# A second buffer for gathered rows in a decode step, and another order of the gathers

## The chip, the cores and the metric

The kernel runs on one core of a Trainium2 chip, as one launch. The metric is its time on the device in microseconds (us), the median of several runs. Engines are named as the profile does: PE (TensorE), DVE (VectorE), ACT (ScalarE), POOL (GpSimd) and SP (SyncE, which here only issues DMAs).

## The reference

One step of a one-layer hybrid decoder: one prompt of 512 tokens and 8 samples of one token each with 4096 past positions. Everything is float32.

```python
h = einsum('btd,de->bte', x, w_in)            # split: HGRN2 part, NSA part, gates
o_hg, S = hgrn2_mix(...)                      # gated linear recurrence, 8 heads of 128
# NSA, per sample: rows = cache_kv[page_table] (past 4096) + the new row
kc = compress(rows[:, :, 0], cmp_w1[0], ...)  # windows of 32 rows, step 16, two-layer net
vc = compress(rows[:, :, 1], cmp_w1[1], ...)
o_cmp, p = cmp_attention(q, kc, vc, qpos)
sel = select_blocks(p, qpos, n_blocks)        # top 16 blocks of 64 rows, per kv head
o_slc = selected_attention(q, blocks(rows[:, :, 2]), blocks(rows[:, :, 3]), sel, qpos)
o_win = window_attention(q, last 512 rows of cache_win and the new one)
o_nsa = (g0 * o_cmp + g1 * o_slc + g2 * o_win) * silu(ngate)
y = LayerNorm(ALPHA * x + concat(o_hg, o_nsa) @ w_out)
```

There are 4 kv heads of 64 with 4 queries each, a model width of 2048, and pages of 128 rows.

## The kernel before, in words

The first stages (prompt, projections) leave `oT`, the transposed outputs of both head groups, [128, 16, 520]. Its first eight columns of 520 are the HGRN2 heads; they are final before the last stage and are next read by its output matmuls. The change lies wholly in that last stage, `decode_output_phase`. It has two parts.

**Decode part.** For each sample `b` of 8 (`NB`) the past rows of the first two kinds go through the compression net. POOL gathers them by indirect DMA (`rows(b, q, par)`, L1485: four gathers of 128 x 2 KB; parity `par` 0 or 1 goes to `X[0]`, in the profile Xr, or `X[1]`, in the profile xT; `q` counts four quarters). PE transposes them in units of four (`turn(Q, u)`, L1534) into one of two PSUM banks `dtb`. ACT empties a bank into `big` (L1799), DVE makes differences (L1900, L1903). Then `product(s, n)` (L1557) runs three matmuls of 512 columns a step `s`, 16 steps a sample. I count in matmuls of `product`: **step t** of a sample's piece, 48 to a sample.

Everything else is a piece with a place in a hand-written list: `AT` gives the step, counted from the start of sample `b`'s 48, at which each engine takes the piece up in its own program order, and `LAST` that of the last sample, whose later pieces lie among the output matmuls (past step 384, each further step is two output matmuls). The pieces of one sample reach over three periods: compression's second layer ("second"), scores, weights, top 16 ("sums" to "bases"), "rows" (DVE writes the list `gi` of chosen rows, L2030), then four "fetch" and "keys" pieces, SCORES, VALUES, the window ("NEWEST", WSCORES, WVALUES) and DONE.

**Chosen rows.** `chosen(b, q)` on POOL issues eight gathers (L1501) of a quarter's rows into `KV`, of which there is one. "fetch q": when the gathers have landed, ACT copies keys to `Kc` (L1856, counts `k_c`) and DVE copies values to `Vg` (L2039 or L2041, counts `v_r`). "keys q": PE transposes `Kc` (L1662), DVE copies the result to `KgT` (L1771). `chosen(b, q)` waits for the copies of the quarter before. `Kc` also serves ACT's `bend` (L1814). POOL's order is: all row gathers of the next sample (`q` 0 to 3, each when PE has turned the old ones), then the four quarters of chosen rows.

**SP's queue** loads each sample's window when the one before is done (`window(b)`, about 1 MB in, 1 MB out), then `w_out` in four pieces of 1 MB (`weights(i)`, L1437) as `X[1]` and `X[0]` come free, then `x` and the norm's weights `gb`, which lies on `w1`'s room.

**Output part.** 16 tiles of 16 matmul pairs (`output(i, k)`, L1575) of `oT` with `w_out`, two PSUM buffers, DVE adds `x` and normalizes. `output_rows` (L1589) does the 8 samples' rows.

Of the kernel before, what the change touches and what calls it, by code (L numbers as in the profile page):

```python
# [18 lines left out]
F32 = mybir.dt.float32  # L19
# [6 lines left out]
P = 128  # L26
# [1204 lines left out]
def decode_output_phase(nc, io, keep):  # L1231
# [16 lines left out]
    NC, NQ4, TILES = D // 512, 4, 9  # L1248
    ident = const[:, C_ID:C_ID + P]
    cache = io["cache"]  # L1250
    with ExitStack() as ctx:
# [14 lines left out]
        KV, Vg = sb("KV", [P, 2, KVH, RUN]), sb("Vg", [P, NT, KVH, DH])  # L1266
        Kc = sb("Kc", [P, 2, KVH, DH])
# [46 lines left out]
        g_in, v_r, k_c, kn_r = sem("g_in"), sem("v_r"), sem("k_c"), sem("kn_r")  # L1314
# [19 lines left out]
            ("second", 2): 51, ("second", 3): 53, "fetch0": 54, "keys0": 55, "mix": 56, "acc": 57,  # L1334
            "fetch1": 63, "keys1": 64, "fetch2": 70, "keys2": 71, "fetch3": 80, "keys3": 81,
# [4 lines left out]
        LAST = {  # L1340
            "SCORES": 83, "SCALE": 85, "TURNED": 87, "VALUES": 89, "NEWEST0": 90, "NEWEST1": 91,
# [14 lines left out]
        def put(key, bank):  # L1356
            place[key], emptied[key] = (bank, had[bank]), (counts[bank], counts[bank] + 1)
            had[bank] += 1
            counts[bank] += 1

# [50 lines left out]
        def _(sp):  # L1411
# [26 lines left out]

            for b in range(NB - 1):
                window(b)  # L1440
            weights(0)
            weights(1)
# [4 lines left out]
            sp.dma_start(gb, io["ln"].unsqueeze(0).to_broadcast([P, 2, D])).then_inc(gb_in, 16)  # L1447
# [4 lines left out]
            sp.wait_ge(v_r, 4 * NB)  # L1452
            sp.dma_start(z[NQT][0:NB], io["x"][SEQ:T]).then_inc(z_in, 16)
# [17 lines left out]
        @block.gpsimd  # L1471
        def _(pool):
            pairs = cache.rearrange("g r (s d) -> (g r s) d", d=2 * KVH * DH)
            heads = cache.rearrange("g r (s d) -> (g r s) d", d=DH)
            for n in range(2):
                nc.gpsimd.memset(qbd[n][:], 0.0).then_inc(init, 1)
            nc.gpsimd.memset(pn[:], 0.0).then_inc(init, 1)
            nc.gpsimd.memset(sc[:], FORCED).then_inc(init, 1)

            def rows(b, q, par):  # L1480
                if b:
                    bank, k = place[NJ * b - 4 + q, 3 - 2 * par]
                    pool.wait_ge(tr[bank], k + 1)
                for r in range(4 * q, 4 * q + 4):
                    pool.indirect_dma_start(  # L1485
                        out=X[par][:, r, :], out_offset=None, in_=pairs,
                        in_offset=bass.IndirectOffsetOnAxis(ap=row[:, 2 * b + par, r:r + 1], axis=0),
                    ).then_inc(x_in[par][q], 16)

            def chosen(b, q):  # L1490

                if q == 0:
                    pool.wait_ge(gi_r, b + 1)
                if 4 * b + q:
                    pool.wait_ge(v_r, 4 * b + q)
                    pool.wait_ge(k_c, 4 * b + q)
                for t in (2 * q, 2 * q + 1):
                    n = P if t < NT - 1 else SL
                    for h in range(KVH):
                        a = h * NT + t  # L1500
                        pool.indirect_dma_start(  # L1501
                            out=KV[0:n, t - 2 * q, h, :], out_offset=None, in_=heads,
                            in_offset=bass.IndirectOffsetOnAxis(ap=gi[b % 2][0:n, a:a + 1], axis=0),
                        ).then_inc(g_in, 16)

            for q in range(4):
                rows(0, q, 0)
            for p in range(NB):
                if p + 1 < NB:
                    for q in range(4):  # L1510
                        rows(p + 1, q, 1)
                        rows(p + 1, q, 0)
                for q in range(4):
                    chosen(p, q)

        @block.tensor
        def _(pe):
# [45 lines left out]
            def output(i, k):  # L1563
# [4 lines left out]
                if k == 0:  # L1568
                    if i == 0:
                        pe.wait_ge(kept, 2 * NB)  # L1570
                    elif i == 1:
                        pe.wait_ge(added, 4 * NB - 1)
                    else:
                        pe.wait_ge(add_r, i - 1)
# [211 lines left out]
        def _(act):  # L1786
# [59 lines left out]
            def fetch(q):  # L1846


                def do(b):
                    act.wait_ge(g_in, 512 * b + 128 * (q + 1))  # L1850
# [5 lines left out]
                    A(Kc[:], KV[:, :, :, 0:DH], ACT.Copy).then_inc(k_c, 1)  # L1856
# [34 lines left out]
        def _(v):  # L1891
# [134 lines left out]
            def rows(b):  # L2026
                v.wait_ge(ix, b + 1)
                if b >= 2:
                    v.wait_ge(g_in, 512 * (b - 1))
# [3 lines left out]
            def fetch(q):  # L2033

                def do(b):
                    v.wait_ge(g_in, 512 * b + 128 * (q + 1))
                    need(v, pv_s, b)
                    if q < 3:
                        V.tensor_copy(Vg[:, 2 * q:2 * q + 2], KV[:, :, :, RUN - DH:RUN]).then_inc(v_r, 1)  # L2039
                    else:  # L2040
                        V.tensor_copy(Vg[:, NT - 2], KV[:, 0, :, RUN - DH:RUN])  # L2041
                        V.tensor_copy(Vg[0:SL, NT - 1], KV[0:SL, 1, :, RUN - DH:RUN]).then_inc(v_r, 1)
# [143 lines left out]
def build(nc, io):  # L2186
    with ExitStack() as ctx:
# [4 lines left out]
        keep = {}  # L2192
        io["v_rows"] = nc.dram_tensor("v_rows", (NB, P), F32, kind="Internal").ap()
# [97 lines left out]
```

## Time and profile before

| what | us |
|---|---|
| three runs | 2334.61, 2340.11, 2341.86 (median 2340.11) |
| profiled execution | 2328.65 |
| its span, first to last instruction | 2326.8 |
| PE busy | 2027.1 (87%) |
| DVE, ACT, POOL busy | 913.9, 707.9, 643.2 |
| mean granted TensorE clock | 0.945 of full |
| last stage, from its first transposes | 1153.7 to the end |
| of it, output part | 2059.8 to the end |

Times are from one execution on the chip. An engine's idle time matters only where the chain of work runs through it. A "busy" PE may be one at a lower clock, which is given as a share of full speed. "remote" and "another core or an unknown queue" on this one core mean that the profile knows when a wait ended but not which instruction ended it.

### The profile page before, as it was taken

How to read it: one execution, taken by the hardware profiler on the slowest of the kernel's cores; microseconds unless marked ns; L12 is line 12 of the kernel's file. 1: busy time of each engine (PE TensorE's matmuls, PEld its weight loads, DVE VectorE, ACT ScalarE, POOL GpSimd, SP SyncE). 2: the span in 40 equal slices, each digit the busy share in tenths (PEclk: the TensorE clock that was granted, in tenths of full speed). 3: DMA queues.
4: the chain of work that ended last, by engine and by line, in shares of the span. 5: the costliest groups of instructions: out<-in, count | busy, mean ns of one | idle time of the engine just before them, and what ended most of it. 6: DMA issues, size and time to landing. Idle time of an engine off the chain costs nothing.

```text
span 2326.8 us, 24655 instructions
## 1 busy us (share of the span) xinstructions
PE 2027.1 (87%) x9303; PEld 1374.4 (59%) x9303; DVE 913.9 (39%) x1813; ACT 707.9 (30%) x1289; POOL 643.2 (28%) x673
## 2 busy tenths in 40 slices
PE   8999999999999999999687585858585857799997
PEld 7888888888888777777444242424242424344442
DVE  0445545545301244444435242525253534432126
ACT  0233312233100132323255353534353534520013
POOL 0000000000010143344455646455555454322000
PEclk9999999999999999999899697979798988999999
DMA  5222222222222211111353525353535353464113
GB/s 196 78 88 72 92 90 82 85 79 73 81 103 95 87 50 42 55 37 37 111 158 106 145 82 165 101 153 113 148 111 152 107 146 112 153 244 149 73 72 146
DMA packets 71684, 248.35 MB, mean 107 GB/s; under 512 B 11572, under 2 KB 29184, under 8 KB 57632
## 3 DMA queue, kind: packets, MB, share of 16 engines
q1 hardware_dynamic: 38056, 136.44, 16.9%
q0 software_dynamic: 32256, 106.46, 16.1%
q10 hardware_dynamic: 1280, 4.23, 0.5%
q8 instruction: 57, 0.93, 0.2%
q14 instruction: 35, 0.29, 0.0%
HBM read 226.46 MB, written 20.63 MB: 106 GB/s over the span
## 4 chain that ended last, share of the span: by engine, by line
PE 21%; DVE 7%; another core or an unknown queue 7%; ACT 6%; issue 5%; POOL 2%; DMA 2%; ACTq 1%; DVEq 0%; POOLq 0%
PE dpH L1575 9%; PE dpH L1557 6%; ACT big L1799 4%; PE dtb L1534 3%; POOL KV L1501 2%; DVE big L1900 2%; DMA KV<-d_cache,gi 2%; DVE big L1903 1%; PE dtb L1662 1%; ACTq L1813 1%; PE dpS L1613 1%; ACT Kc L1856 1%; PE dpS L1712 0%; PE dpK L1607 0%
## 5 line engine op out<-in xcount | busy, mean ns | idle before, releaser
L292 PE MATMUL pj<-xT,strips 128*128 128x260 f32 x2368 | 533.5, 384 | 6.3 <-DMA xT<-d_xT 6.3
L292 PEld LDWEIGHTS pj<-xT,strips 128*128 128x128 f32 x2368 | 446.6, 191 | 72.4 <-issue 6.3
L1799 ACT ACTIVATE big<-dtb 64x512 f32<-64x512 f32 x512 | 302.4, 591 | 403.6 <-PE dtb L1534 185.4
L1501 POOL DMA_INDIRECT KV<-d_cache,gi x256 | 249.1, 973 | 341.6 <-ACT Kc L1856 121.9
L792 PE MATMUL pj<-xT,strips 128*128 128x260 f32 x1216 | 292.2, 388 | 0.0
L1557 PE MATMUL dpH<-big,w 128*128 128x512 f32 x512 | 284.8, 653 | 0.6 <-DVE hs L1917 0.4
L792 PEld LDWEIGHTS pj<-xT,strips 128*128 128x128 f32 x1216 | 222.7, 191 | 59.9 <-issue 30.1
L1018 POOL MEMSET kbd<- 128x128 f32 x1 | 0.2, 204 | 636.3 <-POOLq L126 636.3
L1534 PEld LDWEIGHTS dtb<-const,Xr 128*128 128x128 f32 x512 | 67.9, 154 | 177.6 <-issue 137.8
L1044 POOL TENSOR_SCALAR old<-old,rd 128x128 f32<-128x128 f32 (+3 forms) x116 | 121.9, 1066 | 166.9 <-DVE rd L1153 166.9
L1534 PE MATMUL dtb<-const,Xr 128*128 128x128 f32 x512 | 86.9, 298 | 90.5 <-issue 50.6
L1900 DVE TENSOR_TENSOR big<-big 128x512 f32<-128x512 f32 x128 | 88.1, 688 | 188.6 <-ACT big L1799 125.7
L1557 PE MATMUL dpH<-big 128*128 128x512 f32 x256 | 147.3, 660 | 0.0
L1485 POOL DMA_INDIRECT Xr<-d_cache,row x128 | 131.9, 1030 | 46.8 <-issue 39.0
L1534 PEld LDWEIGHTS dtb<-const,xT 128*128 128x128 f32 x512 | 66.7, 150 | 112.5 <-issue 80.2
L1485 POOL DMA_INDIRECT xT<-d_cache,row x112 | 106.3, 949 | 87.2 <-PE dtb L1534 33.5
L1557 PEld LDWEIGHTS dpH<-big,w 128*128 128x128 f32 x512 | 89.3, 205 | 63.1 <-issue 51.8
L1575 PE MATMUL dpH<-xT,oT 128*128 128x512 f32 x256 | 113.3, 595 | 0.0
L1575 PE MATMUL dpH<-Xr,oT 128*128 128x512 f32 x256 | 113.3, 596 | 0.0
L1534 PE MATMUL dtb<-const,xT 128*128 128x128 f32 x512 | 84.1, 290 | 28.5 <-DVE KgT L1771 16.4
L1662 PE MATMUL dtb<-const,Kc 128*128 128x128 f32 (+1 forms) x128 | 27.5, 327 | 89.6 <-ACT Kc L1856 88.5
L1903 DVE TENSOR_TENSOR big<-big 128x508 f32<-128x508 f32 x128 | 88.3, 690 | 4.4
(299 smaller groups left out, 2294.5 us busy)
## 6 DMA issues: line engine op xcount, KB each, us to landing
strips<-d_w_in SPq DMA_DIRECT2D x60, 1024.0 KB, 5.1
xT<-d_w_out SPq DMA_DIRECT2D x16, 1024.0 KB, 9.4
d_win_sample<-Wt SPq DMA_DIRECT2D x8, 1024.0 KB
Xr<-d_w_out SPq DMA_DIRECT2D x8, 1024.0 KB, 9.6
Wt<-d_win SPq DMA_DIRECT2D x8, 896.0 KB
xT<-d_xT SPq DMA_DIRECT2D x8, 520.0 KB, 8.7
Sold<-d_state SPq DMA_DIRECT2D x8, 512.0 KB, 5.3
vB<-v_rows ACTq DMA_DIRECT2D x8, 512.0 KB, 6.9
```

Source lines behind the costliest of these rows:

```text
L292: mm = nc.tensor.matmul(pj[b][:, a, 0:TH], w[b][:, k, :], xT[:, k, a * TH:(a + 1) * TH], start=(k == 0), stop=(k == KT - 1))
L792: mm = nc.tensor.matmul(bank(s)[:, n, 0:TH], w[s % 2][:, k, :], xT[:, k, n * TH:(n + 1) * TH], start=(k == 0), stop=(k == KT - 1))
L1044: ins = nc.gpsimd.tensor_scalar(p, p, rd[U % 4][:, k:k + 1], None, ALU.mult)
L1485: pool.indirect_dma_start(out=X[par][:, r, :], out_offset=None, in_=pairs, in_offset=bass.IndirectOffsetOnAxis(ap=row[:, 2 * b + par, r:r ...
L1501: pool.indirect_dma_start(out=KV[0:n, t - 2 * q, h, :], out_offset=None, in_=heads, in_offset=bass.IndirectOffsetOnAxis(ap=gi[b % 2][0:n, ...
L1534: mm = nc.tensor.transpose(tb[bank][:, i * P:(i + 1) * P], X[par][:, r, (2 * kind + hp) * P:(2 * kind + hp + 1) * P], ident)
L1557: mm = nc.tensor.matmul(pH[n][:], left, right, start=(j == 0), stop=(j == NJ - 1))
L1575: mm = nc.tensor.matmul(pH[i % 2][:], oT[:, k, t * P:(t + 1) * P], wo[c % 2][:, k, :], start=(k == 0), stop=(k == KT - 1))
L1662: mm = nc.tensor.transpose(tb[bank][:, j * P:j * P + n], Kc[0:n, t, 2 * hp:2 * hp + 2, :].rearrange("p h d -> p (h d)"), ident[0:n, 0:n])
L1799: ins = A(dst[:, :, :, hd], tb[bank][hd * DH:(hd + 1) * DH].rearrange("p (j h n) -> p j h n", j=2, h=2), ACT.Copy)
L1900: V.tensor_tensor(D1[:, s], D2[:, s], Or[:, s], ALU.subtract).then_inc(diff_r, 1)
L1903: V.tensor_tensor(e[:, :, 0:HSUB - 1], e[:, :, 1:HSUB], o[:, :, 0:HSUB - 1], ALU.subtract).then_inc(diff_r, 1)
```

## The change

Chosen rows get two buffers, used in turn: `KV` for quarters 0 and 2, and for 1 and 3 the first five columns of `oT` (samples 0 to 6) or the room of `w1` (sample 7, once all products are done). The five columns, 128 x 10.4 KB = 1.33 MB, are stored to DRAM when the stage begins and loaded again before the output part. `chosen(b, q)` waits for the copies of quarter `q - 2`. POOL's order becomes, for each sample: row quarters 0 and 1 of the next one, chosen quarter 3 of the sample before, row quarters 2 and 3, chosen quarters 0 to 2. The fetch and keys pieces move to later steps, and `gb` is loaded later.

```diff
+    LENT = -(-2 * KVH * RUN // T)
+        lent = oT[:, 0:LENT]
+        KVo = quarter(lent.rearrange("p k t -> p (k t)"))
+        KVw = quarter(w1[:].rearrange("p k n e -> p (k n e)"))
-            ("second", 2): 51, ("second", 3): 53, "fetch0": 54, "keys0": 55, "mix": 56, "acc": 57,
-            "fetch1": 63, "keys1": 64, "fetch2": 70, "keys2": 71, "fetch3": 80, "keys3": 81,
+            ("second", 2): 51, ("second", 3): 53, "mix": 56, "acc": 57, "fetch0": 59, "keys0": 62,
+            "fetch1": 64, "keys1": 66, "fetch2": 72, "keys2": 76, "fetch3": 91, "keys3": 92,
         LAST = {
+            "fetch0": 55, "keys0": 59, "fetch1": 62, "keys1": 63, "fetch2": 70, "keys2": 71, "fetch3": 76, "keys3": 78,
+        def landed(b, q):
+            return g_in[q % 2], 16 * (TAKEN[q % 2] * b + sum(GATHERS[q % 2:q + 1:2]))
+        def buffer(b, q):
+            return KV if q % 2 == 0 else KVo if b < NB - 1 else KVw
+            sp.dma_start(io["lent"], lent).then_inc(lent_out, 16)
             for b in range(NB - 1):
                 window(b)
             weights(0)
+            sp.wait_ge(lent_out, 16)
+            sp.wait_ge(v_r, 4 * (NB - 1))
+            sp.wait_ge(k_c, 4 * (NB - 1))
+            sp.dma_start(lent, io["lent"]).then_inc(lent_in, 16)
             weights(1)
-            sp.dma_start(gb, io["ln"].unsqueeze(0).to_broadcast([P, 2, D])).then_inc(gb_in, 16)
             window(NB - 1)
             sp.wait_ge(mm_r, NQT)
             weights(2)
             sp.wait_ge(ss, NB)
             sp.wait_ge(v_r, 4 * NB)
+            sp.wait_ge(k_c, 4 * NB)
+            sp.dma_start(gb, io["ln"].unsqueeze(0).to_broadcast([P, 2, D])).then_inc(gb_in, 16)
-                if 4 * b + q:
-                    pool.wait_ge(v_r, 4 * b + q)
-                    pool.wait_ge(k_c, 4 * b + q)
+                if 4 * b + q > 1:
+                    pool.wait_ge(v_r, 4 * b + q - 1)
+                    pool.wait_ge(k_c, 4 * b + q - 1)
+                if (b, q) == (0, 1):
+                    pool.wait_ge(lent_out, 16)
+                if (b, q) == (NB - 1, 1):
+                    pool.wait_ge(prod, NSTEP)
             for p in range(NB):
-                if p + 1 < NB:
-                    for q in range(4):
+                for q in range(4):
+                    if p + 1 < NB:
                         rows(p + 1, q, 1)
                         rows(p + 1, q, 0)
-                for q in range(4):
+                    if q == 1 and p:
+                        chosen(p - 1, 3)
+                for q in range(3):
                     chosen(p, q)
+            chosen(NB - 1, 3)
+                        pe.wait_ge(lent_in, 16)
```

ACT's and DVE's copies wait for `landed(b, q)` and read `buffer(b, q)`.

## Rows read from the trace of the kernel before

**Rows 1.** Windows view: us, busy us (instructions) of each engine, PEclk, DMA share, GB/s

```profile
1153.70:1236.30 82.60, 60.06 (x229) 31.40 (x229) 30.07 (x56) 42.79 (x71) 46.67 (x48) 0.88 0.57 166
...
1345.90:1464.60 118.70, 84.08 (x341) 42.21 (x340) 47.89 (x105) 51.61 (x84) 62.69 (x65) 0.87 0.45 130
...
1823.50:1946.40 122.90, 84.08 (x341) 42.17 (x340) 47.91 (x105) 51.61 (x84) 62.96 (x65) 0.86 0.44 126
1946.40:2059.80 113.40, 90.08 (x365) 44.20 (x364) 56.50 (x123) 52.21 (x85) 39.17 (x40) 0.92 0.46 152
2059.80:2326.80 267.00, 253.43 (x789) 108.52 (x787) 88.11 (x120) 35.00 (x52) 26.73 (x28) 0.98 0.35 128
```

**Rows 2.** Waits of PE: the last stage, then one period (us in total, times, longest)

```profile
PE dtb L1662 <- ACT Kc L1856: 88.5, 27, 20.4
...
PE dtb L1662 <- ACT Kc L1856: 9.8, 4, 6.1
```

**Rows 3.** Timeline of PE in one period: start, us, instruction, idle time before it

```profile
1633.97 0.66 PE L1662 MATMUL dtb<-const,Kc 128*128 128x128 f32 x4 [1.91 <-ACT Kc L1856]
...
1652.04 1.11 PE L1662 MATMUL dtb<-const,Kc 128*128 128x128 f32 x4 [6.02 <-ACT Kc L1856]
...
1682.99 1.11 PE L1534 MATMUL dtb<-const,Xr 128*128 128x128 f32 x4 [11.62 <-issue]
```

**Rows 4.** Timeline of POOL, the same period; then line L1501's durations in ns

```profile
1636.64 0.94 POOL L1501 DMA_INDIRECT KV<-d_cache,gi  x1 [9.38 <-DVE Vg L2039]
...
1652.78 0.94 POOL L1501 DMA_INDIRECT KV<-d_cache,gi  x1 [6.42 <-ACT Kc L1856]
...
1686.97 0.95 POOL L1485 DMA_INDIRECT xT<-d_cache,row  x1 [4.65 <-remote]
...
L1501 POOL DMA_INDIRECT KV<-d_cache,gi x256: 893/946/1692, 1246.5 to 2116.0; - x128
```

**Rows 5.** Timelines of PE, ACT and DVE around PE's long stop

```profile
1664.21 0.66 PE L1534 MATMUL dtb<-const,xT 128*128 128x128 f32 x4 [0.62 <-issue]
...
1681.74 1.19 ACT L1799 ACTIVATE big<-dtb 64x512 f32<-64x512 f32 x2 [21.12 <-remote]
...
1686.66 0.42 DVE L1940 COPY kcT<-dpK 128x256 f32<-128x256 f32 x1 [19.95 <-remote]
```

**Rows 6.** Windows view: the long stop, the same work in the last period, a keys wait's end

```profile
1660.10:1686.80 26.70, 9.78 (x31) 4.00 (x30) 3.84 (x10) 1.77 (x4) 16.94 (x18) 0.69 0.60 167
2020.75:2029.40 8.65, 8.03 (x36) 3.81 (x37) 4.13 (x10) 3.43 (x6) 2.14 (x3) 1.00 0.51 160
...
1533.60:1541.00 7.40, 6.71 (x24) 3.64 (x24) 2.76 (x7) 6.96 (x11) 5.57 (x7) 0.78 0.50 159
```

**Rows 7.** Timelines of DVE, PE and ACT around the last quarter's copies and SCORES

```profile
1695.40 0.54 DVE L1771 COPY KgT<-dtb 128x384 f32<-128x384 f32 x1
...
1714.60 0.69 DVE L1903 TENSOR_TENSOR big<-big 128x508 f32<-128x508 f32 x1
...
1712.78 1.78 PE L1613 MATMUL dpS<-KgT,qbd 128*8 128x512 f32 x8
...
1721.66 1.09 PE L1534 MATMUL dtb<-const,Xr 128*128 128x128 f32 x4 [3.45 <-ACT big L1799]
...
1692.26 0.63 ACT L1856 ACTIVATE Kc<-KV 128x512 f32<-128x512 f32 x1
```

**Rows 8.** The stage's start: windows view, and PE's timeline

```profile
1153.70:1163.85 10.15, 1.06 (x9) 0.82 (x8) 3.35 (x4) 2.36 (x4) 8.04 (x9) 0.55 0.89 235
...
1163.85 1.97 PE L1534 MATMUL dtb<-const,Xr 128*128 128x128 f32 x8 [9.10 <-DMA Xr<-d_cache,row]
```

**Rows 9.** The output part's start: timelines of DVE and PE, and the DMA view

```profile
2053.54 0.28 DVE L2021 TENSOR_TENSOR rhs<-base,const 4x32 f32<-4x32 f32 x2
...
2059.82 4.45 PE L1575 MATMUL dpH<-xT,oT 128*128 128x512 f32 x10
...
xT<-d_w_out SPq DMA_DIRECT2D x16, 1024.0 KB, 9.4
```

More of the change, by code:

```diff
@@ L1266, in decode_output_phase @@
         KV, Vg = sb("KV", [P, 2, KVH, RUN]), sb("Vg", [P, NT, KVH, DH])
+        lent = oT[:, 0:LENT]
+        quarter = lambda t: t[:, 0:2 * KVH * RUN].rearrange("p (t h e) -> p t h e", t=2, h=KVH)
+        KVo = quarter(lent.rearrange("p k t -> p (k t)"))
+        KVw = quarter(w1[:].rearrange("p k n e -> p (k n e)"))
         Kc = sb("Kc", [P, 2, KVH, DH])
@@ L1313, in decode_output_phase @@
         w_in, w_out, new_in = sem("w_in"), sem("w_out"), sem("new_in")
-        g_in, v_r, k_c, kn_r = sem("g_in"), sem("v_r"), sem("k_c"), sem("kn_r")
+        g_in, v_r, k_c, kn_r = [sem("g_in0"), sem("g_in1")], sem("v_r"), sem("k_c"), sem("kn_r")
+        lent_out, lent_in = sem("lent_out"), sem("lent_in")
         tr, ev = [sem("tr0"), sem("tr1")], [sem("ev0"), sem("ev1")]
@@ L1359, in put @@
             counts[bank] += 1
+        GATHERS = [2 * KVH] * 4
+        TAKEN = [sum(GATHERS[n::2]) for n in range(2)]
+        def landed(b, q):
+            return g_in[q % 2], 16 * (TAKEN[q % 2] * b + sum(GATHERS[q % 2:q + 1:2]))
+        def buffer(b, q):
+            return KV if q % 2 == 0 else KVo if b < NB - 1 else KVw
         FETCH = "fetch0", "fetch1", "fetch2", "fetch3"
@@ L1493, in chosen @@
                     pool.wait_ge(gi_r, b + 1)
-                if 4 * b + q:
-                    pool.wait_ge(v_r, 4 * b + q)
-                    pool.wait_ge(k_c, 4 * b + q)
+                if 4 * b + q > 1:
[5 more added lines that the diff above has]
+                    pool.wait_ge(prod, NSTEP)
+                KVq = buffer(b, q)
                 for t in (2 * q, 2 * q + 1):
@@ L1501, in chosen @@
                         pool.indirect_dma_start(
-                            out=KV[0:n, t - 2 * q, h, :], out_offset=None, in_=heads,
+                            out=KVq[0:n, t - 2 * q, h, :], out_offset=None, in_=heads,
                             in_offset=bass.IndirectOffsetOnAxis(ap=gi[b % 2][0:n, a:a + 1], axis=0),
-                        ).then_inc(g_in, 16)
+                        ).then_inc(g_in[q % 2], 16)
             for q in range(4):
@@ L1849, in do @@
                 def do(b):
-                    act.wait_ge(g_in, 512 * b + 128 * (q + 1))
+                    act.wait_ge(*landed(b, q))
                     if 4 * b + q:
@@ L1855, in do @@
                     keyed[0] = QUARTERS[q], b
-                    A(Kc[:], KV[:, :, :, 0:DH], ACT.Copy).then_inc(k_c, 1)
+                    A(Kc[:], buffer(b, q)[:, :, :, 0:DH], ACT.Copy).then_inc(k_c, 1)
                 return do
@@ L2028, in rows @@
                 if b >= 2:
-                    v.wait_ge(g_in, 512 * (b - 1))
+                    for n in range(2):
+                        v.wait_ge(*landed(b - 2, 2 + n))
                 V.tensor_tensor(gi[b % 2][:], pK[:, 256:256 + KVH * NT], const[:, C_ROW:C_ROW + KVH * NT],
@@ L2035, in do @@
                 def do(b):
-                    v.wait_ge(g_in, 512 * b + 128 * (q + 1))
+                    v.wait_ge(*landed(b, q))
                     need(v, pv_s, b)
+                    KVq = buffer(b, q)
                     if q < 3:
-                        V.tensor_copy(Vg[:, 2 * q:2 * q + 2], KV[:, :, :, RUN - DH:RUN]).then_inc(v_r, 1)
+                        V.tensor_copy(Vg[:, 2 * q:2 * q + 2], KVq[:, :, :, RUN - DH:RUN]).then_inc(v_r, 1)
                     else:
-                        V.tensor_copy(Vg[:, NT - 2], KV[:, 0, :, RUN - DH:RUN])
-                        V.tensor_copy(Vg[0:SL, NT - 1], KV[0:SL, 1, :, RUN - DH:RUN]).then_inc(v_r, 1)
+                        V.tensor_copy(Vg[:, NT - 2], KVq[:, 0, :, RUN - DH:RUN])
+                        V.tensor_copy(Vg[0:SL, NT - 1], KVq[0:SL, 1, :, RUN - DH:RUN]).then_inc(v_r, 1)
                         need(v, sw, b)
@@ L2192, in build @@
         keep = {}
+        io["lent"] = nc.dram_tensor("lent", (P, 5, T), F32, kind="Internal").ap()
         io["v_rows"] = nc.dram_tensor("v_rows", (NB, P), F32, kind="Internal").ap()
```

## The prediction, made before the changed kernel was run

> **What bounds the kernel now.** I read the clock and span first (one core, span 2326.8 us), then the page's busy shares, and then cut the decode stage into equal pieces of work with the windows view. A period here runs from one sample's first transposes to the next one's. PE is 73% busy or less in a period and 95% busy in the output stage behind it [rows 1]. So the output stage has nothing to give, and a period has: the five full ones take 118.7 to 122.9 us for 83 to 84 us of PE work. Period 0, which has no chosen rows yet, takes 82.6.
>
> Next the waits of PE: the transposes of chosen keys (L1662) wait 88.5 us for ACT's copy of KV into Kc [rows 2]. One of those waits, 20.4 us, belongs to something else (below). The other 68.1 us are 9.7 us in each of seven periods; a single period asked alone gives 9.8. Its timeline shows who: the third quarter waits 6.0 us, the second 1.9 [rows 3]. POOL's own timeline gives the cause. It issues eight gathers of 1.25 us each (0.946 at the median and 0.30 between), then sits 9.4 and 6.4 us until KV is copied out [rows 4]. The third quarter is gathered too late for its place in PE's order, with only one buffer to gather into.
>
> The same timeline shows a larger loss that the change does not speak of. In a period PE stops for 11.6 us at a transpose [rows 3], which waits for ACT to empty a bank. ACT had sat 21.1 us before it, waiting for transposes that PE began at 1664.21; DVE sat 20.0 us at kcT [rows 5]. PE's signals arrive late. From 1660.1 to 1686.8 the work done is what the last period does in 8.65 us at full clock [rows 6]. So 26.7 - 8.65, with the slots that follow, is about 19 us lost per period. What differs: the last period has no row gathers. In the others POOL runs from 1652.78 without a pause through chosen quarter 3 and row quarters 0 and 1 (24 gathers), and the stretch ends as POOL pauses at 1686.97 [rows 4]. I call this the slow stretch. It follows long runs of gathers; that they cause it is argued, not shown.
>
> **The change, part by part.**
>
> (a) Second buffer, pieces moved later. chosen(b, q) now waits for the copies of quarter q-2, and the copies stand later in the order. Place of each: step t counts the product's matmuls from the sample's start, 48 in a period; fetch0 goes from 54 to 59, fetch1 from 63 to 64, fetch2 from 70 to 72, fetch3 from 80 to 91. A period of 92 us (119.5 less the 19 of the slow stretch and the 8.8 worked out here) is 1.9 us a step, the tightest case. From the list gi (step 45) POOL needs 20 us for quarters 0 and 1; fetch0 comes at 14 steps, 27 us. Quarter 2 runs to 37, fetch2 is at 51. Row quarters 0 and 1 run to 57, chosen 3 to 67, fetch3 is at 87. Each is early by 10 us or more, so the waits at L1662 go. Gross gain: 9.7 us, plus 7.4 x (1 - 0.78) = 1.6 us of half clock behind the wait [rows 6], 11.3 in all. Lower bound: only the third quarter's wait and its clock, 6.0 + 1.6 = 7.6. Upper: 12.9, if the turn 1.5 us behind keys1 goes too. Of TensorE's clock, the granted 0.78 over 7.4 us is a mix of the two levels, 1.2 and 2.4 GHz, after a stop. I take 11.3: all four waits have the same cause.
>
> (b) fetch3 now lies three steps before SCORES. DVE's queue there is full: differences to 1714.60 + 0.69, and PE began the scores at 1712.78 [rows 7]. Behind the differences now comes the copy of the last quarter's keys, 0.54, and in front of them ACT's Kc copy, about 0.63. Scores begin at about 1716.5, 3.7 late. Some 1.2 of it comes back, since PE waits 3.45 at 1721.66 for the softmax anyway [rows 7]. Net cost 2.5 a period, bounds 0 (absorbed wholly) and 3.7. gi itself comes 1.2 later, which POOL's slack hides; without that slack it would delay rows by as much.
>
> Net (a) - (b): 8.8 us a period, bounds 3.9 to 12.9. Seven periods have it (1 to 7): 61.6.
>
> (c) oT's first five columns, 1.33 MB, are stored at the stage's start, ahead of window(0) on SP's queue. The DMA engines move 235 GB/s at 89% there, and PE waits 9.10 us for the first rows [rows 8]. Taken in full, 1.33 MB is 5.7 us; if the gathers' own pace of issue sets the landing, 0. I take 4, nearer the upper end, as the engines are nearly full. Nothing else waits: chosen(0, 1), which now waits for the store, comes 100 us later.
>
> (d) The reload waits on SP for the copies of sample 6's last quarter, step 43 of the last period. DVE gets there after bases, at 2053.8; PE wants oT at 2059.82 [rows 9]. 1 MB loads land in 9.4 us at the median, four queued; alone, 1.33 MB should take less. Cost 1 us, bounds 0 and 2053.8 + 0.7 + 9.4 - 2059.8 = 4. Behind it on SP wait the second load of w_out (first needed 64 matmul pairs later, some 57 us), then x and the last window; gb moves behind the last SCORES, used only after output tile 9. All are covered by the output tiles.
>
> (e) The order of gathers. Their number and price stay: 64 x 1.25 = 80 us a period. Chosen 2, row quarters 0 and 1, chosen 3 and row quarters 2 and 3 now form one run of 60 us, if nothing stops POOL. The slow stretch began 8 us into a run of 24 gathers before: the run from 1652.78, ACT idle from 1660.6 [rows 4, 5]. In the new order window traffic meets row quarters 0 and 1. If it begins there, some 17 us into the run, and lasts until POOL must stop at row quarter 2 for PE's own transposes, it lasts some 27 us at the same rate: again about 19 lost. I take 0 for this part. The ends: -19 (it goes) and +15 a period (it starts 8 us into the run and fills row quarters 2 and 3 too). Six periods (1 to 6) have it.
>
> A rule that speaks to (e): the Trainium skill, "SBUF — State Buffer", section "SBUF: two separate sides", says that a DMA and a compute operation cannot slow each other. By it neither end of (e) would hold and the sum would be as I take it; the rows of the slow stretch, at 167 GB/s, look otherwise [rows 6].
>
> Sum: -61.6 + 4 + 1 + 0 = -56.6. The profiled run took 2328.65 us and its span 2326.8; so 2272.0 for that run. The runs' median is 2340.11, 11.5 above. **Predicted for the median: 2283.5 us**, -2.4%. The period becomes about 111 us.
>
> **The rivals.**
> - The slow stretch goes, because POOL's run meets other work of PE. For it: a gather run of 16 in period 0 leaves that period at 82.6 us. Against: the run gets longer. -6 x 19 more: 2170 us; POOL's 80 us plus its wait for fetch0 (7 us) still fit the 92 us period.
> - It shrinks by half, as its first 10 us fall on steps with fewer round trips. 2283.5 - 57 = 2227.
> - It eats the gain: it lasts longer by what the keys' waits were, so that PE's idle time only moves. 2325 to 2345.
> - Slower: the unbroken run of 60 us holds PE's signals longer. Place: row quarters 2 and 3, steps 78 to 90. Price: up to 15 a period, 90 in all, 2374 us. It decides when over 28 us a period are lost in slow stretches (19 now, plus 57 / 6). For it: the stretch ended only when POOL paused [rows 4]. Against: POOL must wait for PE's transposes before row quarters 2 and 3, which breaks the run.
> - The change doesn't do what it says: the second and third quarters still come late, since POOL is busy elsewhere. Speaks against: POOL idles 9.4 + 6.4 us exactly there. 2335 to 2345.
>
> **How the numbers follow.** Forecast case 0.45, its own range 2255 to 2312: (a) and (b) at 3.9 and 12.9 a period give 2318 and 2255, (c) and (d) add -5 to +5. Half 0.18, gone 0.14, gain eaten 0.10, slower 0.08, no effect 0.05. The range for 8 in 10 leaves out most of the gone case and the larger part of the slower one, whose ends lie at 2170 and 2374: 2195 to 2350. A measurement of this kernel tells about 0.3% (7 us) from no change. Faster by more: 0.45 + 0.18 + 0.14 + 0.05 of the eaten case = 0.82. Within: 0.08 (0.05 of the eaten case, 0.03 of no effect). Slower: 0.10 (0.08, and 0.02 of no effect).
>
> **What the profile would show.** PE's waits at L1662 for ACT fall from 88.5 us to under 15. POOL's waits for Kc and Vg within a period shrink to one, before chosen quarter 2. (b) shows as a wait of 3 to 4 us at L1613 in each period. (c): the first wait for Xr is 13 us in place of 9.1. (d): a gap of about 1 us before the first L1575. (e): ACT's and DVE's waits that the profile puts to "remote" stay near 173 and 112 us if the stretch keeps its size; near zero and the period is 92, near double and the change loses. The prediction is wrong above all if (e) is not 0.

## The result

The changed kernel takes 2313.98 us at the median of four runs (2309.71 to 2317.52) beside 2340.39 for the kernel before on the same chip: ratio 0.9891 [0.9867, 0.9915], 1.1% faster. The forecast was 2.4%. Run twice more, on two chips (e14, e17), it came to 0.9860 [0.9837, 0.9883] and 0.9934 [0.9912, 0.9955]. The profiled execution took 2317.52 us, its span 2315.7.

Windows view of the changed kernel, cut by sample as [rows 1]:

```profile
1153.00:1235.30 82.30, 60.31 (x230) 32.07 (x229) 30.03 (x56) 42.84 (x71) 47.23 (x48) 0.83 0.59 183
...
1338.50:1446.80 108.30, 84.16 (x341) 41.47 (x340) 47.59 (x104) 51.45 (x84) 61.19 (x63) 0.91 0.45 137
1446.80:1576.70 129.90, 94.28 (x342) 45.71 (x341) 48.14 (x105) 51.55 (x84) 65.51 (x67) 0.80 0.42 124
1576.70:1687.20 110.50, 88.91 (x342) 44.18 (x341) 46.68 (x102) 50.26 (x82) 61.10 (x63) 0.85 0.45 135
...
1922.70:2043.70 121.00, 96.17 (x370) 46.77 (x368) 57.28 (x128) 52.67 (x86) 38.27 (x39) 0.89 0.36 117
2043.70:2315.70 272.00, 254.71 (x788) 108.56 (x788) 87.92 (x119) 35.02 (x52) 27.22 (x28) 0.99 0.37 141
```

Periods 2 and 4 take 108.3 and 110.5 us, near the forecast 111, but period 3 has 129.9, period 7 has 121.0 (113.4 before), and the output part 272.0 (267.0). Now the waits of PE over the last stage:

```profile
PE dtb L1566 <- ACT big L1832: 55.4, 29, 5.9
PE dtb L1566 <- issue: 43.0, 23, 5.0
...
PE dtb L1566 <- DMA Xr<-d_cache,row: 12.1, 1, 12.1
...
PE dpS L1646 <- DVE KgT L1804: 7.8, 5, 1.9
...
PE dtb L1695 <- ACT Kc L1889: 2.9, 4, 1.3
```

The keys' transposes (now L1695) wait 2.9 us in place of 88.5 [rows 2]. The turn's transposes (now L1566) wait for ACT and for "issue" instead, and the scores (L1646) for the last quarter's keys. ACT's waits put to "remote", which carried the slow stretch, are still there (172.9 us in 25 before, longest 24.6):

```profile
ACT big L1832 <- remote: 182.5, 33, 13.9
```

The late signals also reach a new place. The timelines of DVE and PE at the start of period 4 show it, in the softmax of the chosen rows. PE was through with the transposes that DVE copies at 1600.7, and DVE was free from 1603.5, but it starts only as POOL's run of chosen quarters 0 and 1 (1587.7 to 1607.4) ends, and PE waits for DVE:

```profile
1607.24 0.27 DVE L2098 COPY PTg<-dtb 128x112 f32<-128x112 f32 x1 [3.75 <-remote]
...
1607.64 1.76 PE L1745 MATMUL dpS<-Vg,PTg 128*16 128x256 f32 x16 [2.31 <-DVE PTg L2099]
```

### The profile page after: what moved, and what is told of

Same layout as the page of the kernel before. It is cut to its first block and busy times, and to the rows that moved or that the text cites. A ratio compares the mean times of both kernels' runs of the same rounds, so it can differ in the third digit from the quotient of the medians.

```text
span 2315.7 us, 24657 instructions
## 1 busy us (share of the span) xinstructions
PE 2058.5 (89%) x9303; PEld 1384.1 (60%) x9303; DVE 913.1 (39%) x1813; ACT 707.3 (31%) x1289; POOL 647.1 (28%) x673
## 3 DMA queue, kind: packets, MB, share of 16 engines
q1 hardware_dynamic: 38344, 139.10, 17.4%
## 5 line engine op out<-in xcount | busy, mean ns | idle before, releaser
L1832 ACT ACTIVATE big<-dtb 64x512 f32<-64x512 f32 x512 | 302.8, 591 | 410.1 <-remote 182.5
L1589 PE MATMUL dpH<-big,w 128*128 128x512 f32 x512 | 294.7, 672 | 7.2 <-DVE hs L1950 6.6
L1530 POOL DMA_INDIRECT KV<-d_cache,gi x128 | 126.6, 989 | 257.8 <-DVE gi L2064 105.8
L1566 PEld LDWEIGHTS dtb<-const,Xr 128*128 128x128 f32 x512 | 71.2, 162 | 178.4 <-issue 125.5
L1566 PE MATMUL dtb<-const,Xr 128*128 128x128 f32 x512 | 94.2, 315 | 82.6 <-ACT big L1832 38.6
L1566 PEld LDWEIGHTS dtb<-const,xT 128*128 128x128 f32 x512 | 65.5, 149 | 130.4 <-issue 93.8
L1566 PE MATMUL dtb<-const,xT 128*128 128x128 f32 x512 | 83.9, 289 | 50.0 <-issue 21.0
L1608 PE MATMUL dpH<-xT,oT 128*128 128x512 f32 x256 | 114.3, 597 | 1.5 <-issue 1.2
L1530 POOL DMA_INDIRECT oT<-d_cache,gi x112 | 105.3, 940 | 34.1 <-issue 34.1
```

The lines of the kernel that those rows point to most:

```text
L1530: pool.indirect_dma_start(out=KVq[0:n, t - 2 * q, h, :], out_offset=None, in_=heads, in_offset=bass.IndirectOffsetOnAxis(ap=gi[b % 2][0:n, ...
L1566: mm = nc.tensor.transpose(tb[bank][:, i * P:(i + 1) * P], X[par][:, r, (2 * kind + hp) * P:(2 * kind + hp + 1) * P], ident)
L1589: mm = nc.tensor.matmul(pH[n][:], left, right, start=(j == 0), stop=(j == NJ - 1))
L1608: mm = nc.tensor.matmul(pH[i % 2][:], oT[:, k, t * P:(t + 1) * P], wo[c % 2][:, k, :], start=(k == 0), stop=(k == KT - 1))
L1832: ins = A(dst[:, :, :, hd], tb[bank][hd * DH:(hd + 1) * DH].rearrange("p (j h n) -> p j h n", j=2, h=2), ACT.Copy)
```

## The experiments

Each ratio is to the kernel before on the same chip. Five chips were used, one for each of e1 to e4 (before: 2337 us), e5 to e8 (2336), e9 to e12 (2192), e13 to e16 (2334), and e17 and e18 (2334). On four of them the kernel before takes the same time; I call them **A**. The one of e9 to e12 I call **B**. Expectations in microseconds written for A do not fit B. The A chips are not quite alike for other kernels: the changed one took 2305.78 us (e14) and 2318.93 (e17) on two of them, where the kernel before took 2334.43 and 2334.06. So a difference between kernels on two A chips is known to some 13 us only.

| run | what | ratio [95%] |
|---|---|---|
| e1 | before, no row gathers | 0.9471 [0.9443, 0.9499] |
| e2 | changed, no row gathers | 0.9492 [0.9464, 0.9520] |
| e3 | changed, old order | 0.9886 [0.9835, 0.9938] |
| e4 | before, new places | 1.0195 [1.0156, 1.0234] |
| e5, e15 | second buffer alone | 0.9753 [0.9731, 0.9776], 0.9760 [0.9743, 0.9778] |
| e6 | changed, a break in POOL's run | 1.0105 [1.0080, 1.0130] |
| e7 | before, half the bytes | 0.9988 [0.9973, 1.0004] |
| e8 | before, a pause for POOL | 1.0045 [1.0028, 1.0062] |
| e9 (B) | changed, old places | 0.9954 [0.9937, 0.9971] |
| e10 (B), e18 | buffer, last quarter late | 0.9775 [0.9750, 0.9800], 0.9901 [0.9879, 0.9922] |
| e11 (B), e16 | buffer, quarters 1 and 2 later | 0.9740 [0.9717, 0.9764], 0.9761 [0.9744, 0.9778] |
| e12 (B) | buffer, no row gathers | 0.9768 [0.9750, 0.9786] |
| e13 | before, again | 0.9989 [0.9978, 0.9999] |
| e14, e17 | changed, again | 0.9860 [0.9837, 0.9883], 0.9934 [0.9912, 0.9955] |

Where the time of a period goes shows in the steps. The table gives the mean of periods 2 to 6 in us, from the starts of `product`'s matmuls in each trace; the sum is a whole period, counted from the first of these.

| trace | steps 0 to 7 | 8 to 21 | 22, 23 | 24 to 31 | 32 to 41 | 42 to 47 | sum |
|---|---|---|---|---|---|---|---|
| before | 20.1 | 26.6 | 9.6 | 35.1 | 17.0 | 11.7 | 120.1 |
| changed | 23.2 | 29.8 | 2.4 | 21.5 | 22.8 | 17.8 | 117.5 |
| e4, before, new places | 18.8 | 29.9 | 2.5 | 20.5 | 42.7 | 14.5 | 128.9 |
| e8, before, a pause | 19.7 | 26.5 | 10.1 | 24.6 | 17.4 | 24.6 | 123.0 |
| e15, buffer alone | 24.7 | 27.0 | 2.6 | 26.8 | 16.6 | 12.7 | 110.5 |
| e16, quarters 1 and 2 later | 24.9 | 24.9 | 2.2 | 29.9 | 16.3 | 12.4 | 110.5 |
| e18, last quarter late | 23.7 | 26.9 | 3.1 | 27.8 | 13.7 | 19.9 | 115.1 |
| e10 (B), the same | 20.1 | 25.8 | 2.6 | 16.3 | 13.6 | 13.7 | 92.0 |

### e1, e2, e7, e8: what holds the signals up

e1 and e2 leave the row gathers of samples 2 to 7 out; the products work on old rows.

```diff
-                for r in range(4 * q, 4 * q + 4):
+                for r in range(4 * q, 4 * q + 4 if b < 2 else 4 * q):
```

> The kernel before, with the row gathers of samples 2 to 7 left out (PE turns the rows of samples 0 and 1 again and no longer waits for later ones), so its outputs for those samples are not the reference's. Theory G (runs of gathers on POOL make PE's signals late): periods 1 to 6 lose their slow stretch, some 20 us each, the wait of the third quarter's keys stays; periods near 98 us, total 2215 to 2235 us. Theory Q (the late signals and PE's stops come from the full queues of ACT, DVE and PE, not from gathers): periods near 119 us, total within 10 us of 2340.

> The changed kernel with the row gathers of samples 2 to 7 left out in the same way. Theory G: only the run of chosen quarters 0 and 1 is left to make signals late; periods near 95 us, no more alternation of long and short ones, total 2190 to 2215 us, below the kernel before without row gathers by the 8.8 us a period that were forecast (60 us), or by less if the doubled chosen run costs something. Theory Q: total within 10 us of 2314.

e1: 2212.75 us, 125 less. ACT's "remote" waits fall from 172.9 us to:

```profile
ACT big L1799 <- remote: 19.0, 6, 5.2
```

So on an A chip the slow stretch needs the row gathers. The changed kernel without them (e2, 2217.48) is no faster than e1, where 2190 to 2215 was expected. It keeps more late signals, from the chosen gathers alone:

```profile
ACT big L1832 <- remote: 82.9, 11, 12.4
```

e7 gathers to 64 of the 128 partitions, half the bytes by as many gathers:

```diff
-                        out=X[par][:, r, :], out_offset=None, in_=pairs,
+                        out=X[par][0:m, r, :], out_offset=None, in_=pairs,
```

> The kernel before, with the row gathers of samples 2 to 7 on 64 partitions in place of 128 (half the rows are left out, so the outputs differ), the same number of gathers. If late signals follow the bytes or descriptors in flight: the slow stretch goes, total near that of the kernel without row gathers, 2215 to 2240. If they follow the number of gathers that POOL issues in a run: total 2330 to 2345.

2335.95 us, no change: it is not the bytes that the row gathers move. e8 makes row quarter 1 wait for PE's turn of quarter 2, which breaks the run of 24 gathers:

```diff
-                    bank, k = place[NJ * b - 4 + q, 3 - 2 * par]
+                    bank, k = place[NJ * b - 4 + max(q, 2) if q else NJ * b - 4, 3 - 2 * par]
```

> The kernel before, with one wait changed: row quarter 1 is issued only when PE has turned the rows of quarter 2, step 30, where before it was issued at once behind row quarter 0. It breaks POOL's run of 30 us behind chosen quarter 3 into 20 and 10. Theory G, run length decides: of the 19 us lost a period half or more comes back, total 2260 to 2300. If only the number of row gathers in a period counts: within 8 us of 2340.

2347.31 us, just inside the second expectation, where the number of row gathers counts. Steps 24 to 31 take 24.6 us in place of 35.1, but steps 42 to 47 take 24.6 in place of 11.7: PE now stops at steps 42 and 43 as well, where the held-back gathers end (POOL issues 20 of them without a pause from step 32 or 34). The loss follows the gathers.

### e3 to e6: places, order and buffer apart

e3 is the changed kernel with POOL's old order (all rows of the next sample, then quarters 0 to 3). e4 is the kernel before with the new `AT` and `LAST` only.

> The changed kernel (two buffers, new places of fetch and keys) with POOL's old order: all four row quarters, then the four chosen quarters. Theory G: the runs are 20 us (chosen 0 and 1) and then chosen 2, chosen 3, rows 0, rows 1 with short waits between, as long as in the new order; total within 15 us of 2314. Rival (the new order is what made the gain or the loss): the old order gives 2280 us if the order was what ate the gain, or 2340 and more if it was what made it.

> The kernel before (one buffer, old order on POOL) with only the places of fetch and keys moved as in the change. If the second buffer is what takes the keys' waits away: waits at the keys' transposes of 4 to 6 us a period stay, the scores' wait of 3 to 4 us is added, total 2330 to 2350. If the later places alone take them away: total 2300 to 2320, as the changed kernel.

e3: 2308.47 us, so with the new places the order is worth nothing that can be told between these chips. e4: 2383.04 us, 46 slower, where neither expectation went above 2350. The late places by themselves, with one buffer, take most of the keys' waits away; ACT's copy of the keys is waited for 5.6 us, and 19.0 at the same transposes are for ACT's emptying of a bank:

```profile
PE dtb L1663 <- ACT big L1800: 19.0, 8, 6.0
...
PE dtb L1663 <- ACT Kc L1857: 5.6, 6, 2.1
```

But POOL's run in front of the slow stretch grows from 24 gathers to 32 (1558.0 to 1598.3 in period 3), and PE stops for 29 us in that period, in two pieces, instead of the 11.6 of [rows 3]. A wait that goes is not yet time gained.

e5 keeps both the old places and the old order: second buffer, store and reload alone.

```diff
-            ("second", 2): 51, ("second", 3): 53, "mix": 56, "acc": 57, "fetch0": 59, "keys0": 62,
-            "fetch1": 64, "keys1": 66, "fetch2": 72, "keys2": 76, "fetch3": 91, "keys3": 92,
+            ("second", 2): 51, ("second", 3): 53, "fetch0": 54, "keys0": 55, "mix": 56, "acc": 57,
+            "fetch1": 63, "keys1": 64, "fetch2": 70, "keys2": 71, "fetch3": 80, "keys3": 81,
```

> The second buffer alone: the changed kernel with the places of fetch and keys and POOL's order as before the change. Theory G with the queue cost of the late places: the keys' waits go (7 us a period), no scores' wait, but chosen quarters 0 and 1 make one run of 20 us and bring late signals of 3 to 6 us a period there, and chosen 2 and 3 with rows 0 and 1 another, longer one; periods near 113 to 118, total 2300 to 2330. Rival (the loss is all from the later places and the new order): 2270 to 2285, the forecast.

2280.4 us; the rival was right. On one and the same chip (e14, e15) it is 27 us below the changed kernel. Periods 1 to 7 take 109.7 to 114.3 us, the output part 269.1. Two periods and the output part of its repeat e15, by the windows view:

```profile
1444.10:1553.60 109.50, 83.61 (x341) 42.12 (x340) 48.18 (x105) 51.61 (x84) 63.26 (x65) 0.89 0.49 141
1553.60:1666.10 112.50, 86.02 (x341) 42.39 (x340) 48.13 (x105) 51.61 (x84) 62.49 (x65) 0.86 0.48 138
2000.00:2267.40 267.40, 253.45 (x789) 108.52 (x787) 88.10 (x120) 35.05 (x52) 27.16 (x28) 0.98 0.34 128
```

The periods are even; none of periods 1 to 7 runs past 114.3, where the changed kernel has three of 120 or more in its first trace, two in e17 and none in e14 (118.3 at the most). e6 is the changed kernel in which chosen quarter 1 waits for the copies of quarter 0, so that the run of quarters 0 and 1 is broken:

```diff
+                if q == 1:
+                    pool.wait_ge(v_r, 4 * b + 1)
+                    pool.wait_ge(k_c, 4 * b + 1)
```

> The changed kernel with one wait added: chosen quarter 1 is issued only when quarter 0 has been copied, which breaks the run of two chosen quarters but makes quarter 1 land some 13 us after fetch0's place, 4 us late for fetch1's. Theory G: the 5 to 10 us of late signals between steps 2 and 8 go, a keys' wait of about 4 us comes back, and periods 3 and 5 lose their excess; total 2285 to 2310. Rival (that stretch is DVE's and ACT's full queue): the stretch between steps 2 and 8 stays and the wait is added; 2325 to 2345.

2363.72 us, above both expectations. The late signals of steps 2 to 8 did go (steps 0 to 7 take 18.5 us), but everything that POOL issues came later, and that cost more: 12.1 us at steps 22 and 23, 2.4 in the changed kernel.

### e9 to e12: a chip without late signals

> The changed kernel with the pieces at their old steps and POOL's new order: the fourth of the four mixes of places and order, beside the changed kernel (2314 us), new places with the old order (2308) and old places with the old order (2280). Theory I, places and order belong together: in the new order POOL takes up chosen quarter 3 only after row quarters 0 and 1 of the next sample, which wait for PE's own transposes to about step 24 of the period. Chosen 3 then lands near step 34 to 40, while its piece stands at step 32, so PE waits 5 to 15 us there in each of six or seven periods: 2315 to 2385, with those waits at the keys' transposes. Rival N, the order is indifferent here too, as it was with the new places: 2275 to 2290.

> The second buffer alone (2280 us), and of the new places only those of the last quarter (fetch3 91, keys3 92) for samples 0 to 6. This is term (b) of the prediction by itself: the copies of the last quarter's keys in front of the scores, 3.6 us a period as seen in the changed kernel. Theory B, term (b) is nearly all that the new places cost (28 us between the second buffer alone and new places with old order): 2298 to 2308, with a wait of 3 to 4 us at PE's scores in each period. Rival L, the new places cost mainly through PE's late signals, by where quarters 0 to 2 put the chosen gathers: 2275 to 2290, the wait at the scores being made good at the softmax behind it.

> The second buffer alone (2280 us), and of the new places only those of quarters 1 and 2 (fetch1 64, keys1 66, fetch2 72, keys2 76) for samples 0 to 6. There the keys' waits are still 32 us in 19, since ACT's copy is taken up one step ahead of PE's transposes. Theory K: with 2 and 4 steps between copy and transposes half of that goes and nothing comes back: 2260 to 2275, the best so far. Rival L, these places push the chosen gathers and so the row gathers to where PE's signals are needed: 2285 to 2305.

> The second buffer alone, with the row gathers of samples 2 to 7 left out as in the kernel before (2213 us) and the changed one (2217 us). Theory B, what the changed kernel pays for its later places is paid without row gathers too (3.6 us a period in front of the scores): the second buffer alone is then faster than both, 2180 to 2200. Rival M, the second buffer is worth something only through what it does to the gathers' order in time, and nothing without row gathers: 2208 to 2220.

The edits of e10 and e11 are single lines on e5 (samples 0 to 6; in e12 the edit of e1 on e5):

```diff
-            "fetch1": 63, "keys1": 64, "fetch2": 70, "keys2": 71, "fetch3": 80, "keys3": 81,
+            "fetch1": 63, "keys1": 64, "fetch2": 70, "keys2": 71, "fetch3": 91, "keys3": 92,
```

```diff
-            "fetch1": 63, "keys1": 64, "fetch2": 70, "keys2": 71, "fetch3": 80, "keys3": 81,
+            "fetch1": 64, "keys1": 66, "fetch2": 72, "keys2": 76, "fetch3": 80, "keys3": 81,
```

Chip B runs the kernel before in 2191.74 us, 145 less than A. In none of the four traces has the decode part a wait put to "remote". The row gathers seem to cost nothing there: 2142.15 us without them (e12), 2141.73 (e10) and 2134.28 (e11) with them, though in e10 and e11 some pieces stand at other steps than in e12. Two samples' windows of e10, then one of e11:

```profile
1295.90:1387.70 91.80, 78.22 (x342) 40.17 (x341) 47.86 (x105) 51.55 (x84) 67.19 (x68) 0.96 0.60 178
...
1479.60:1571.00 91.40, 76.93 (x342) 39.38 (x341) 47.68 (x105) 51.55 (x84) 63.93 (x65) 0.98 0.60 172
```

```profile
1489.50:1580.90 91.40, 78.81 (x342) 39.23 (x341) 47.92 (x105) 51.62 (x84) 64.19 (x65) 0.96 0.58 169
```

The same work takes 91 us, POOL is as busy as on A (64 to 67 us here, 61 to 66 above) and the DMA engines move more per second. The gathers themselves are no quicker: `KV` 981 ns at the mean in e10, 973 in the trace of before. In e10 POOL issues 56 gathers without a pause, from 1530.96 to 1602.86, and no signal is late. The last quarter's late place costs no time in the period (91.4 and 91.4). e9, the new order with the old places, gives nearly all of the gain back (2182.96 us): chosen quarter 3 comes behind row quarters 0 and 1, and PE waits for it at its old step.

```profile
PE dtb L1694 <- ACT Kc L1888: 60.6, 21, 9.9
```

So order and places belong together, as theory I had it.

### e13 to e18: back on A

> The kernel before, unchanged, for its profile on this chip. Two kinds of chip have been seen: with late signals (2337 to 2340 us, periods of 119) and without (2192 us). Theory C, the late signals belong to the chip together with the row gathers: where the kernel takes 2192 us, its trace has periods of 98 to 101 us, no wait of ACT or DVE over 15 us put to remote in the decode part, and the keys' waits of 8 to 10 us a period are still there (60 to 90 us in all). Rival D, the difference between chips is one of all transfers (faster gathers or clock): then POOL's 1.25 us a gather is shorter too, and the keys' waits shrink with it to under 40 us.

> The changed kernel, unchanged. On a chip with late signals 2308 to 2318 us (0.989 of before), as measured. On a chip without them, theory C: what is left of the change is (a) -9 to -11 a period and (b) up to +3.7, with (c) and (d), so 2130 to 2150 us where before takes 2192 (0.972 to 0.981), with even periods of 91 to 93. Rival O, the new order costs by itself even there (chosen quarter 3 behind row quarters 0 and 1): 2150 to 2190, with waits of PE for chosen rows.

> The second buffer alone (old places, old order). On a chip with late signals 2275 to 2290 us (0.975), as measured. Without them, theory C: with and without row gathers it should be the same, and that ran in 2142 us, so 2135 to 2150; places and order then cost nothing or little, and the changed kernel lies within 10 us of it. Rival: under 2130, then the new places' term (b) costs 3.6 us a period there as well.

> The second buffer with the new places of quarters 1 and 2 only. Without late signals 2130 to 2140 us, as measured (0.974). With late signals, theory K: the second buffer's 2280 less half the keys' waits, 2260 to 2275. Rival L: these places push chosen and row gathers to where signals are needed, 2285 to 2305.

> The changed kernel, unchanged. On a chip with late signals a repeat (0.986 to 0.989 of before). On one without (before 2192 us), theory C: only terms (a) to (d) act, 2130 to 2150 us (0.972 to 0.981), periods of 91 to 93. Rival O, the new order costs by itself even there: 2150 to 2190.

> The second buffer alone, with only the last quarter's pieces at their new steps 91 and 92. On a chip without late signals a repeat (0.9775 of before). On one with them, theory B: the copies in front of the scores are most of what the new places cost, 0.982 to 0.988 of before (2293 to 2308 us where before takes 2335). Rival L: the places of quarter 0 (and 1, 2) cost it through the late signals, 0.973 to 0.979 here.

All six fell on A chips. e13 has the late signals again, so theory C was tested on A chips only:

```profile
ACT big L1799 <- remote: 170.7, 23, 22.3
```

e16 ties with e15 (2279.1 and 2278.34 us), against theory K: PE's keys' waits fall from 32.1 us to 22.5, the stop in steps 24 to 31 grows by 3.1 us a period and eats it. e18 has the last quarter's place alone, which cost nothing inside the periods on B. On A it takes the second buffer from 0.976 to 0.990, 2278.34 to 2313.06 us, more than the 2308 expected. The two ran on different chips, and the changed kernel took 27.4 us more than e15 on e15's and 5.9 more than e18 on e18's, so the place costs some 22 to 35 us and most of the distance between e15 and the changed kernel.

First, what A and B do with one and the same program. The same place, first e18 on A, then e10 on B:

```profile
1639.34 0.94 POOL L1530 DMA_INDIRECT oT<-d_cache,gi  x1 [9.43 <-DVE Vg L2071]
...
1648.56 0.60 PE L1692 MATMUL dtb<-const,Kc 128*128 128x128 f32 x4
...
1658.10 0.94 POOL L1509 DMA_INDIRECT Xr<-d_cache,row  x1 [0.30 <-issue]
1662.05 0.69 DVE L1801 COPY KgT<-dtb 128x512 f32<-128x512 f32 x1 [9.90 <-remote]
1662.11 1.28 ACT L1844 ACT_TABLE_LOAD   x1 [14.39 <-remote]
1662.79 1.11 PE L1563 MATMUL dtb<-const,xT 128*128 128x128 f32 x4 [12.77 <-DVE KgT L1801]
```

```profile
1540.18 0.60 PE L1692 MATMUL dtb<-const,Kc 128*128 128x128 f32 x4
1540.88 1.28 ACT L1844 ACT_TABLE_LOAD   x1 [1.54 <-PE dtb L1692]
...
1542.85 0.67 DVE L1801 COPY KgT<-dtb 128x512 f32<-128x512 f32 x1
1543.58 0.98 PE L1563 MATMUL dtb<-const,xT 128*128 128x128 f32 x4 [1.94 <-DVE KgT L1801]
```

On B the transposes that start at 1540.18 free ACT at 1540.88. On A those of 1648.56 free ACT and DVE only at 1662.1, 13.5 us on and 3 us behind POOL's last gather of the run. PE then stands 12.8 us. Such a stop comes once in each of periods 2 to 6 of e18, at steps 24 and 25, of 10.1 to 12.8 us. It is not the late place that makes it: e15 has it at the same transposes, of 9.7 to 11.2 us.

```profile
1511.38 0.60 PE L1691 MATMUL dtb<-const,Kc 128*128 128x128 f32 x4
1511.82 1.02 PE L1585 MATMUL dpH<-big 128*128 128x512 f32 x2
1522.58 1.12 PE L1562 MATMUL dtb<-const,xT 128*128 128x128 f32 x4 [9.74 <-issue]
```

What the late place costs stands in the table's steps 42 to 47, where the copies now lie: 19.9 us in e18, 12.7 in e15, and 13.7 for the program of e18 on B. Steps 32 to 41 give 2.9 back. In e18 POOL issues 12 gathers there without a pause (1559.7 to 1574.9), in e15 it pauses after 8, and as they end DVE and ACT start late, just before the copies:

```profile
1574.77 0.21 DVE L2020 COPY sc<-dpK 4x62 f32<-4x62 f32 x1 [4.80 <-remote]
...
1576.92 4.85 ACT L1829 ACTIVATE big<-dtb 64x512 f32<-64x512 f32 x8 [3.10 <-remote]
```

## Why the prediction came out as it did

The sign held, and the keys' waits went as forecast; that the slow stretch would stay as it was did not hold. The gain was taken at 56.6 us and is 26.

**(a)** The keys' waits went, 88.5 to 2.9, and steps 22 and 23, where the third quarter's keys were waited for, take 7.2 us less a period. I took 11.3, as if every wait removed were time gained; on A part of it came back as other waits (e4, e16). With the old places the waits shrink only in part:

```profile
PE dtb L1691 <- ACT Kc L1885: 32.1, 20, 3.8
```

That kernel gives 56 us both times (e5, e15). It lands on the forecast of 2283.5, but by luck, from another sum. By the table (e15 beside the kernel before) a period has 7.0 us less at steps 22 and 23, 8.3 less at steps 24 to 31, where the slow stretch shrank with POOL's run from 24 gathers to 16, and 4.6 more at steps 0 to 7, where the run of chosen quarters 0 and 1 is new. There is no term (b) in it, and (e) is not 0.

**(c)** The first wait for Xr is 12.1 us in place of 9.10 [rows 8]: 3, where I took 4.

**(b)** In the changed kernel the scores (L1646, 1587.35) start 10.65 us into period 4, against 8.7 before (1593.39 in a period from 1584.7); the wait for KgT shows as 1.91 us, not 3 to 4. They then run 3.38 us for the 1.78 of [rows 7]. On B, after that same wait of 1.91, they run 1.78 (e10, 1490.22), and the period is none the longer. On A the last quarter's place costs 34.7 us by the medians of e18 and e15, some 22 if the difference of their chips is taken off; 6.7 of these are in the output part (274.1 against 267.4). The rest is 2 to 4 us in each of seven periods, beside the 2.5 that I took.

**(e) is the step that failed, and it took part of (a) with it.** I left the slow stretch's change at 0, from a guess of where it would begin and end. By the table it moved everywhere: in the changed kernel steps 24 to 31 take 13.6 us less a period, and all others but 22 and 23 take 18.2 more (steps 0 to 21 6.3, steps 32 to 41 5.8, steps 42 to 47 6.1). That is (b) and (e) together, 4.6 a period where I had 2.5. The other part of the miss is in (a), 7.2 for 11.3: steps 8 to 21, where the second quarter's wait was, take 3.2 more and not less. A period of this trace gained 2.6 us in place of 8.8. I priced the moved pieces by their work in the queues of DVE and PE alone, where on A a long run of gathers holds up whatever stands beside it.

The order by itself is worth 0 with the new places (e3: 0.9886 beside 0.9860 to 0.9934 for the changed kernel). The signs that I had named read so: "remote" on ACT stayed near 173 (182.5), but DVE's for kcT fell from 112.4, and PE's idle time spread over the turn's transposes:

```profile
DVE kcT L1973 <- remote: 28.0, 6, 7.8
```

The rule of the Trainium skill, "SBUF — State Buffer", section "SBUF: two separate sides", says that a DMA and a compute operation cannot slow each other. For the bytes moved the runs agree: with half of them (e7) nothing changed. But by it I would have kept the 0, and the time between a matmul's end and another engine's start does depend on the gathers on A (e1: -125 us); on B no wait of the decode part shows it.

**(d)** I took 1 us and held all loads behind the reload to be covered. The gap at the first output matmul is small, as said:

```profile
PE dpH L1608 <- DMA oT<-lent: 0.2, 1, 0.2
```

The cover of the loads was thinner than I took it. The reload waits for the copies of sample 6's last quarter, step 43 of the last period, and `x` stands behind it on SP. DVE waits for `x` in the output part, its copy of the last sample's keys is late behind that, and PE waits for the copy:

```profile
DVE big L2147 <- DMA big<-d_x: 11.9, 1, 11.9
```

```profile
PE dtb L1719 <- DVE KgT L1804: 2.5, 1, 2.5
```

In e10 PE waits 4.7 us for that copy, at the scores. The output part says when it happens: 267.0 to 267.7 us in e4, e9, e11, e12, e15 and e16, which have the early place or no reload, and 270.2 to 275.0 in e2, e3, e6, e10, e14, e17, e18 and the changed kernel, which have a late place and the reload. e5 stands between with 269.1. It is 5 us in the changed kernel (3 to 8 in all of these), against my bounds of 0 to 4.

**The rivals.** "The slow stretch is gone, period 92" is what a B chip shows: 91.4 us in e10 and e11. On A none of the rivals came as written. The nearest is the gain eaten, by half, and so PE's idle time in part only moved. What I named as making the prediction wrong, (e) not 0, did so, through the second buffer and the places and not through the order. (The forecast case's own range was given as 2255 to 2312; its sum gives 2318.)

**The sum, corrected for A:** second buffer alone -56 with (c) in it, last quarter's place in the periods +15 to +28, the late reload +7: -34 to -21. Measured were -26 (the first result), -29 (e14) and -15 (e17). On e17's chip the buffer with the late last quarter (e18) has -21, so 6 us more come from the other places and the order.

**Left open.** Neither the changed kernel nor e5 ran on B, so the full price of the change there is unknown; e10 and e11 put the buffer's worth at 50 and 57 us of 2192. The kernel before was timed on B but not profiled, and B is one chip. Why a signal of PE is late on A and not on B no run shows. That a longer run of gathers makes a longer stop is shown by one run that leaves every piece in its place (e8); the others from which it is read (e4, e15) differ in more than that.

## What to carry to other kernels

Take the second buffer and leave the pieces where they are: 2278 us on A with no edit to the schedule, against 2306 with it on the same chip (e15, e14). A piece that is moved later moves what hangs on its count too, here the gathers behind it and, in the last period, a reload with `x` behind it, so each later place is to be followed through every queue and priced by itself. Judge a move by the time of each stretch of work and not by the wait that it was to remove: e4 took the waits at the keys' transposes from 88.5 us to 25 and lost 46 us. And run a schedule tuned to within a per cent on more than one chip: the later place of the last quarter cost 22 to 35 us on A (e18 against e15), and on B the kernel that has it lay 7 us behind one that hasn't (e10, e11), most of it in the output part (273.4 and 267.0 us).

## What the runs showed of the hardware

- Chips differ, and not by clock or transfer rate alone. The same kernel before took 2334 to 2340 us on the A chips and 2191.74 on B, with gathers of the same length (981 ns at the mean in e10, 973 before).
- On A other engines see PE's signals 10 us and more late while GpSimd issues indirect gathers: 14.39 us of idle ACT in e18, 24.6 at the longest in the kernel before. Leaving the row gathers out takes this away (e1: 0.9471), halving their bytes doesn't (e7: 0.9988). On B 56 gathers in a row made none late.
- On A the loss was the larger, the longer the run of gathers that ends in row gathers. Beside e10's steps on B, 16 in a row cost 8.3 and 10.5 us (e8 and e15, steps 24 to 31), 24 cost 18.8 (before, the same steps), 32 cost 29.1 (e4, steps 32 to 41). The run of 16 chosen gathers at the period's start cost 4.6 (e15, steps 0 to 7).
- A gather of 128 rows costs POOL about 0.95 us and 0.30 to the next; one of 64 rows costs about 0.90 (medians of 903 and 899 ns in e7's trace), with the kernel's time unchanged.
